# A 128x512 attention loop with three dense steps a round, and gates finished on VectorE where they are made

## The reference, cut to what matters

```python
h = rmsnorm(x, norm1_g[l])
...
o = diff_attention(q, k, vb, lam, slopes)
o = rmsnorm(o, sub_norm_g[l]) * (1.0 - lam_init)
y_b = o.transpose(0, 2, 1, 3).reshape(bsz, s, B_WIDTH)

gates = jax.nn.sigmoid(h @ w_gate[l] + b_gate[l])
g_a, g_b = jnp.split(gates, 2, axis=-1)
merged = g_a * (y_a @ w_up_a[l]) + g_b * (y_b @ w_up_b[l])
x = x + merged @ w_out[l]

h2 = rmsnorm(x, norm2_g[l])
```

## Time and profile before

| | us |
|---|---|
| median of 3 runs | 1771.48 |
| lowest, highest | 1768.0, 1773.71 |
| the profiled execution | 1772.76 |
| its span | 1770.7 |
| PE busy | 1523.5 (86%) |
| DVE busy | 948.3 (54%) |
| ACT busy | 714.9 (40%) |

### The profile page before, as it was taken

The page is one execution under the profiler, slowest core; times in us unless marked ns, Lnnn a source line. Parts: engine busy times, 40 slices in busy tenths (PEclk is TensorE's granted clock), DMA queues, the critical chain, the costliest instruction groups (busy, mean ns, idle before and its releaser), DMA issues.

```text
span 1770.7 us, 17596 instructions
## 1 busy us (share of the span) xinstructions
PE 1523.5 (86%) x7159; PEld 1147.0 (65%) x7159; DVE 948.3 (54%) x1301; ACT 714.9 (40%) x1043; POOL 68.2 (4%) x80
## 2 busy tenths in 40 slices
PE   5999997798786963899999991989697899999999
PEld 4888775586565842555555551868585877678887
DVE  3444246623763445788888874675545535321334
ACT  4333334424443220666666662244322215652231
POOL 1000000000000000111011101000000000000000
PEclk9999998998997986899999996999897988999999
DMA  6422221122104430999999984220101003002241
GB/s 197 168 96 75 96 73 66 68 75 72 70 26 161 152 119 23 307 327 340 331 336 335 329 294 156 72 71 26 47 1 48 1 24 119 1 1 72 95 143 48
DMA packets 80348, 224.01 MB, mean 127 GB/s; under 512 B 9044, under 2 KB 10182, under 8 KB 76167
## 3 DMA queue, kind: packets, MB, share of 16 engines
q1 hardware_dynamic: 71558, 193.73, 32.3%
q0 software_dynamic: 6144, 20.71, 3.5%
q10 hardware_dynamic: 2560, 8.39, 1.3%
HBM read 200.00 MB, written 22.81 MB: 126 GB/s over the span
## 4 chain that ended last, share of the span: by engine, by line
PE 59%; DVE 25%; ACT 11%; DMA 2%; issue 2%; SPq 1%; POOL 0%; DVEq 0%; POOLq 0%; ACTq 0%
PE PS L502 14%; PE PS L504 14%; PE PS L503 14%; DVE wlo L1152 7%; DVE htlo L1152 5%; PE PS L928 4%; ACT whi L1950 3%; PE PS L499 3%; DVE ylo L1152 2%; ACT work L1950 2%; PE PS L1077 2%; ACT yhi L1950 2%; PE PS L1068 1%; ACT hthi L1950 1%; DVE work L1561 1%
## 5 line engine op out<-in xcount | busy, mean ns | idle before, releaser
L1152 DVE TENSOR_TENSOR wlo<-raw,whi 128x2048 fp32r<-128x2048 f32 x74 | 169.1, 2291 | 356.3 <-ACT whi L1950 356.3
L1950 ACT ACTIVATE whi<-raw 128x2048 fp32r<-128x2048 f32 x74 | 141.2, 1912 | 334.9 <-PE PS L504 333.5
L499 PE MATMUL PS<-consts,work 128*128 128x128 f32 (+1 forms) x652 | 100.7, 298 | 125.9 <-DVE work L1178 53.2
L502 PE MATMUL PS<-whi,hthi 128*128 128x512 f32 x480 | 200.1, 417 | 9.2 <-ACT work L1950 6.4
L502 PE MATMUL PS<-hthi,whi 128*128 128x512 f32 x480 | 198.3, 413 | 5.1 <-ACT scratch L1950 2.8
L503 PE MATMUL PS<-wlo,hthi 128*128 128x512 f32 x480 | 190.9, 398 | 0.0
L504 PE MATMUL PS<-whi,htlo 128*128 128x512 f32 x480 | 190.8, 398 | 0.0
L504 PE MATMUL PS<-hthi,wlo 128*128 128x512 f32 x480 | 190.0, 396 | 0.0
L503 PE MATMUL PS<-htlo,whi 128*128 128x512 f32 x480 | 189.5, 395 | 0.0
L499 PEld LDWEIGHTS PS<-consts,work 128*128 128x128 f32 (+1 forms) x652 | 85.2, 182 | 155.1 <-DVE work L1178 54.4
L1950 ACT ACTIVATE work<-PS 128x512 f32<-128x512 f32 (+3 forms) x204 | 103.3, 531 | 88.6 <-PE PS L992 51.2
(11 more groups left out here) (320 smaller groups left out, 2600.3 us busy)
## 6 DMA issues: line engine op xcount, KB each, us to landing
raw<-in_w_in SPq DMA_DIRECT2D x44, 1024.0 KB
raw<-in_w SPq DMA_DIRECT2D x80, 512.0 KB
scratch<-in_w SPq DMA_DIRECT2D x48, 512.0 KB
raw<-in_w SPq DMA_DIRECT2D x19, 1024.0 KB
scratch<-in_w SPq DMA_DIRECT2D x13, 1024.0 KB
raw<-in_w_gate SPq DMA_DIRECT2D x8, 1024.0 KB
raw<-in_w_out SPq DMA_DIRECT2D x8, 1024.0 KB
y_scratch<-work ACTq DMA_DIRECT2D x32, 256.0 KB, 7.1
```

What stands on the lines that cost most here:

```text
L499: return e.transpose(o, i, ident[0:n, 0:n])
L502: e.matmul(o, lh, rh, start=start, stop=False)
L1152: tt(lo, raw_place(j), as_f32(hi), SUB).then_inc(*ve.mark("lo", j))
L1950: return e.activation(o, i, f, bias=bias, scale=scale)
```

## The change

The loop has 20 rounds and advances the generator three times in each. What is left of it runs behind the loop, and only then comes `finish` of the last head. DVE has its third advance behind `combine`.

ACT no longer copies a gate chunk; it writes exp(-(x + bias)), with the negated bias made once in `nbg`. DVE adds 1 and takes the reciprocal (`gate_sum`), one step into the next chunk, the last one in the last gap. In the first half DVE then multiplies `mg` by it (`gated`) and nothing is stored. In the second half POOL stores it after the reciprocal. The merge loads one set instead of two, and has no sigmoids.

```diff
-    gate_dram = nc.dram_tensor("gate_scratch", [2, KD, P, SEQ], F32, kind="Internal").ap()
+    gate_dram = nc.dram_tensor("gate_scratch", [KD, P, SEQ], F32, kind="Internal").ap()
...
-    g2p = small(KD)
+    g2p, nbg = small(KD), small(2 * KD)
...
# tensor
-            for n in range(STEPS + 5):
+            for n in range(STEPS + 4):
                 if n < STEPS:
                     scores(half, n)
-                next(beside, None)
                 next(beside, None)
                 if 0 <= n - 2 < STEPS:
                     turn_weights(half, n - 2)
...
             for _ in beside:
                 pass
+            finish(half, STEPS - 1)
...
# vector
+            ts(nbg, bg, -1.0, None, MUL).then_inc(*ve.mark())
...
+        def gate_sum(half, k):
+            tmp = merge_tmp[:, k % 2, :]
+            on.wait_ge(*ac["out", ("ga", "gb")[half], k // HB, k % HB])
+            ts(tmp, tmp, 1.0, None, ADD).then_inc(*ve.mark())
+            settle()
+            e.reciprocal(tmp, tmp).then_inc(*ve.mark("gate", half, k))
+
+        def gated(k):
+            settle()
+            on.wait_ge(*ac["out", "ua", k // HB, k % HB])
+            tt(mg[:, k, :], mg[:, k, :], merge_tmp[:, k % 2, :], MUL).then_inc(*ve.mark("gated", 0, k))
+
         def beside_attention(half):
             for b in range(2):
                 for c in range(HB):
+                    k = b * HB + c
                     for kk in range(KD):
+                        if kk == 1 and k:
+                            gate_sum(half, k - 1)
+                        if kk == 2 and k and half == 0:
+                            gated(k - 1)
                         yield
                 for step in range(GAP):
                     if step in (0, 2):
                         split()
+                    if step == 4 and b:
+                        gate_sum(half, KD - 1)
+                        if half == 0:
+                            gated(KD - 1)
                     yield
...
-            for n in range(STEPS + 5):
+            for n in range(STEPS + 4):
                 if n < STEPS:
                     scores(half, n)
-                next(beside, None)
                 next(beside, None)
                 if 0 <= n - 3 < STEPS:
                     normalise_head(half, n - 3)
                 next(beside, None)
-                next(beside, None)
                 if 0 <= n - 1 < STEPS:
                     combine(half, n - 1)
+                next(beside, None)
                 if 0 <= n - 5 < STEPS:
                     finish(half, n - 5)
             for _ in beside:
                 pass
+            finish(half, STEPS - 1)
...
# vector, merge_second
-                    on.wait_ge(*ac[event, "gate"])
+                    on.wait_ge(*(gate_got["all"] if name == "ub" else ac[event, "gate"]))
+                    if name == "ub":
+                        on.wait_ge(*gate_put[k % 2][KD - 2 + k % 2])
...
-        for k in range(KD):
-            on.wait_ge(*ac["gate a", k])
-            tt(mg[:, k, :], mg[:, k, :], gate_a[:, k, :], MUL).then_inc(*ve.mark())
-        ve.also("first merged 1")
...
# scalar, gate_chunk
-            if half or k > 1:
-                on.wait_ge(*gate_put[k % 2][half * KD + k - 2])
-            else:
-                on.wait_ge(*ve["dist"])
-                on.wait_ge(*yz_put["all"])
-            act(merge_tmp[:, k % 2, :], inside(name, b, c), ACT.Copy).then_inc(*ac.mark("out", name, b, c))
+            on.wait_ge(*ve["gains"])
+            on.wait_ge(*yz_put["all"])
+            if half == 0 and k > 1:
+                on.wait_ge(*ve["gated", 0, k - 2])
+            elif half:
+                on.wait_ge(*(gate_put[k % 2][k - 2] if k > 1 else ve["gated", 0, KD - 2 + k]))
+            act(merge_tmp[:, k % 2, :], inside(name, b, c), ACT.Exp, bias=nbg[:, half * KD + k:half * KD + k + 1],
+                scale=-1.0).then_inc(*ac.mark("out", name, b, c))
...
# scalar, the same rounds as above, and
-        on.wait_ge(*gate_got["all"])
-        for k in range(KD):
-            act(gate_a[:, k, :], gate_a[:, k, :], ACT.Sigmoid, bias=bg[:, k:k + 1]).then_inc(*ac.mark("gate a", k))
-        for k in range(KD):
-            act(gate[:, k, :], gate[:, k, :], ACT.Sigmoid, bias=bg[:, KD + k:KD + k + 1]).then_inc(*ac.mark())
-        ac.also("merged", "gate")
...
# gpsimd
-        for half, name in enumerate(("ga", "gb")):
-            for k in range(KD):
-                on.wait_ge(*ac["out", name, k // HB, k % HB])
-                e.dma_start(gate_dram[half, k], merge_tmp[:, k % 2, :]).then_inc(*gate_put[k % 2].mark(half * KD + k))
+        for k in range(KD):
+            on.wait_ge(*ve["gate", 1, k])
+            e.dma_start(gate_dram[k], merge_tmp[:, k % 2, :]).then_inc(*gate_put[k % 2].mark(k))
...
# sync
-        e.dma_start(gate_a, gate_dram[0].rearrange("k p n -> p k n")).then_inc(*gate_got.mark("first"))
-        e.dma_start(gate, gate_dram[1].rearrange("k p n -> p k n")).then_inc(*gate_got.mark("all"))
+        e.dma_start(gate, gate_dram.rearrange("k p n -> p k n")).then_inc(*gate_got.mark("all"))
...
-        on.wait_ge(*ve["first merged 1"])
+        on.wait_ge(*pe["ub", 1, HB - 1])
+        on.wait_ge(*ve["attention"])
         e.dma_start(xw, xv).then_inc(*xw_got.mark("all"))
```

More of the change, by code:

```diff
@@ L274, in build @@
     gate = W[:, 0:2, :].rearrange("p a n -> p (a n)").rearrange("p (k n) -> p k n", k=KD)
-    gate_a = W[:, 2:4, :].rearrange("p a n -> p (a n)").rearrange("p (k n) -> p k n", k=KD)
     h2t = W[:, 2:4, :].rearrange("p a n -> p (a n)").rearrange("p (k n) -> p k n", k=KD)
@@ L2575, in sync @@
         e.dma_start(wr[:, :, NG:], w_re[0].rearrange("(k p) n -> p k n", p=P)).then_inc(*wr_got.mark("all"))
-        on.wait_ge(*gate_put[0][2 * KD - 2])
-        on.wait_ge(*gate_put[1][2 * KD - 1])
-        e.dma_start(gate_a, gate_dram[0].rearrange("k p n -> p k n")).then_inc(*gate_got.mark("first"))
-        e.dma_start(gate, gate_dram[1].rearrange("k p n -> p k n")).then_inc(*gate_got.mark("all"))
+        on.wait_ge(*gate_put[0][KD - 2])
+        on.wait_ge(*gate_put[1][KD - 1])
+        e.dma_start(gate, gate_dram.rearrange("k p n -> p k n")).then_inc(*gate_got.mark("all"))
         first_out = unit["wo", 0][0]
```

## The result

| | before | after |
|---|---|---|
| median, us | 1770.28 (4 runs) | 1803.32 (4 runs, 1799.35 to 1808.44) |
| ratio after to before | | 1.0181, 95% interval 1.0157 to 1.0205 |
| profiled execution, us | 1772.76 | 1805.49 (span 1803.8) |
| DVE busy, us | 948.3 | 1006.9 |
| ACT busy, us | 714.9 | 703.5 |

The change makes the kernel 33 us slower; 1804 us was forecast. Three windows over the changed part answer to the earlier trace rows: stretch, length, busy time and instructions of PE, PEld, DVE, ACT and POOL, granted clock, DMA share and GB/s.

What follows compares the result with a forecast made beforehand. Loops bound by a ring of PE scores, DVE maximum, ACT exponentials, DVE combine and PE transposes, with DVE late. 1772.76 + 7.6 + 40.4 - 13.7 - 1.3 = 1805.8, less 1.3: 1804 us; range 1785 to 1824.

Steps and rivals of the forecast that it cites:

- Part 1: Attention loops: three dense steps (three matmuls each) a round instead of four cost +3.8 us a half, +7.6 us for both.
- Waits for L1294: In each loop, PE's waits for the last DVE instruction of combine grow by 7.1 us a half.
- the end: Behind each loop, the 7.8 us wait for the scaled last head becomes 4.5 us for the split: 3.3 us gained.
- The sixteen dense steps: Behind the loop, sixteen dense steps (10.9 us) run before the last head's transposes and cover its square, root and scaling.
- Part 2: Gates on DVE in the loops: ten gate sums of 3.67 us plus 3.6 us of products, together +40.4 us.
- the exposure: In each loop, five gate sums stand between a maximum and combine, each paid in full: 18.4 us a half.
- no cover: DVE's idle time before combine hides none of the gate sums; up to 5 us a half kept for the low end.
- My check against the sigmoids: ACT's gate exponential costs nothing over the 0.60 us copy, since sigmoids of that shape take 9.91 / 16 = 0.62 us.
- The clock: Rival: five longer PE waits a half each add up to 1 us through slower matmuls, 1814 us; chance 0.08.
- Part 3: Merge: w_up_b product loses its idle PE and slow matmuls, -13.7 us; the second norm's table load goes, -1.3 us.
- The slope: DVE's 128x512 reciprocal: 6 ns for each further element, from medians at 2 and 4 elements, gives 3.2 us.
- the two medians: Reciprocals of 166 ns for 2 elements a partition and 178 ns for 4, compared because both start after a wait.

Runs made afterwards that it cites:

- e_act3c: Changed kernel (three steps a round) with gates finished on ACT, plus, in the middle gap, high parts behind a round's exponentials and low parts behind a combine: 1763.59 us, ratio 0.9921.
- the rounds alone: Kernel before with only the changed rounds (three dense steps a round, 20 rounds, rest behind the loop), gates as before: 1782.95 us, ratio 1.0042.
- e_act4c: Kernel before's rounds, gates finished on ACT, end splits behind the last head's scaling, middle-gap DVE low parts three advances after ACT's high parts: 1755.43 us, ratio 0.9873.
- e_act4: Changed kernel with gates finished on ACT (exponential, logarithm, exponential) and the rounds of before, four advances a round: 1762.26 us, ratio 0.9902.
- e_sizes: Changed kernel with each chunk's reciprocal made in 1, 2, 4, 8 or 16 pieces, 512 to 32 elements a partition: 1803.48 us in one run.

## Why the prediction was right

**Part 1, the rounds.** Forecast +3.8 us a half, measured +4.7 and +4.2 us. Waits for L1294 grew by 8.0 us in the first half (7.1 forecast), the end gained 3.4 us (3.3 forecast), and the late thing there is the split's low part after 4.4 to 4.5 us, as forecast. Wrong was the place: I spread the growth over all waiting rounds, and three fifths of it sat in the two rounds with splits. With the splits apart the first loop keeps about 0.8 us of the cost and the second about 3.6 us, by the estimate from e_act3c, so how much the other rounds pay stays open. The sixteen dense steps in front of the last head's transposes were also a miscount: sixteen advances lie behind the loop and six of them are empty; from the last product with v on it is fourteen steps, which still cover the head's chain.

**Part 2, the gates.** The term was 40.4 us, all of it waits. Against the rounds alone the loops grew by 20.2 and 13.8 us, 34.0 us, and only 13.6 + 9.4 = 23.0 us of that is idle time of PE; the other 6.6 + 4.4 = 11.0 us are longer busy time (the clock, below). The reciprocal was nearly right (3.35 us for 3.2), the exposure was not: of five gate sums in the second loop (5 x 3.82 = 19.1 us) 9.4 us show as idle time of PE, 13.8 us with its longer busy time. Two steps of the forecast failed. I placed every sum between a maximum and a `combine`; the ones at steps 17 and 47 of the generator stand behind the `combine`, ahead of the next scores. And "no cover" was too hard: DVE's waits in front of L1288 are 10.8 and 11.5 us with the rounds alone and 8.9 and 9.3 us with the gate sums, so some 2 us a half were hidden there. (The fall from the 13.2 us of the earlier trace rows is larger, but about half of it comes with the rounds.) Where the rest of the 19.1 us went was not followed. ACT's exponential with a bias takes 687 ns, not the 597 of the copy that I put at nothing; it is 0.09 us, 16 times. My check against the sigmoids misread their row: 9.91 / 16 = 0.62 us is the distance from one to the next, and one takes 708 ns. ACT's groups by form in the first loop of e_act4c show it, with the logarithm above it and the second exponential below:

```profile
L1961 ACT ACTIVATE scratch<-scratch,consts 128x512 f32<-128x512 f32 x8 | 5.8, 723 | 0.3
L1961 ACT ACTIVATE scratch<-PS,smalls 128x512 f32<-128x512 f32 x8 | 5.5, 687 | 15.4 <-PE PS L503 15.4
L1961 ACT ACTIVATE scratch<-scratch 128x512 f32<-128x512 f32 x8 | 5.0, 631 | 0.3
```

**The clock** was a rival with a chance of 0.08, and its 10 us are there: PE is busy 6.7 us longer in the first loop and 4.4 us in the second for the same matmuls. Without it the waits for L1294, +21.4 us in the first half, less the end's 3.3 us, would give +18.1 us; 24.9 us were measured. The sum did not reach the rival's 1814 us because the waits grew by less than forecast. The argument against it, that slow work in a waiting round is free, did not hold. A reason may be that some of it runs ahead of the scores on which DVE waits; which of the slow work counts was not isolated.

**Part 3, the merge.** Forecast -13.7 us, measured 59.00 - 46.15 = -12.9 us (-13.1 us in e_act4), and the table load -1.29 us. Nothing took the place of the wait: the gates' load was issued 8.7 us after PE began the product (590.65 against 581.91), and PE never waited for the unit issued behind it.

**The slope.** 3.2 us came from 12 ns between 2 and 4 elements, and e_sizes says that this was luck in part. A line of 6.36 ns an element and 95 ns gives 108 and 121 ns there. The two of 4 elements take 178 ns, those of 2 elements 106 to 168 ns by what stands in front of them, so a fixed time that depends on the neighbour covers the slope at these sizes. My reason for the two medians was wrong as well: I said that both operations start after a wait, but the two of 4 elements have 0.0 us idle before them. The sign of the slope was sound (a streaming operation adds 2 ns), its size was not to be trusted as far as I did. By the Trainium skill's repeat count of 8 (VectorE: DVE Perf Modes, First, the fixed hardware budget), read as eight passes, an estimate is 4.3 us; a pass is put at the 1.05 ns that an element adds to a product here (692 ns for 512 and 161 ns for 4). The trace does not agree: it has 3353 ns, about six such passes.

**The sum.** +8.9 for the rounds (7.6 forecast), +34 for the gates (40.4), -14.2 for the merge and the norm (15.0) is +28.7 us. The 33 us of the medians hold 4 us more, no more than executions differ by in the unchanged stretches. That 1804 us was forecast and 1803 us came is luck: the waits behind the gates were put at 40.4 us and are 23.0 us, the clock was put at nothing and costs 11.0 us, and the 4 us fill the rest. What the prediction had right is that a 128x512 reciprocal on DVE takes over 3 us, that it stands in the ring, and that its cost is larger than what the merge gains.

## What to carry to other kernels

An engine that is busy for 65% of a loop has little room if it sits in the loop's ring: of 19.1 us put between steps of the ring 13.8 us were paid here, whatever the busy share says, so new work belongs on the engine that idles in the ring, or behind the step that others wait for. Look up a new instruction's price per element before moving a function to another engine; here the same gate costs 3.8 us on DVE or two ACT instructions of 0.6 to 0.7 us, and all of the gates on ACT lengthen a half by 2 us. And take the cost of a stage of preparation (here loads and sixteen sigmoids behind the loop) apart from the rearrangement that is meant to hide it: the merge gained its 13 us with either.

## What the runs showed of the hardware

DVE's RECIPROCAL on float32 costs 6.36 ns for each element of a partition from 32 to 512 elements; 128x512 take 3353 ns where a product of the same shape takes 692 ns, almost five times as long. For 2 elements it takes 106 ns right behind another, long reciprocal and 167 ns after a wait. ACT's ln and exp in place over 128x512 take 723 and 631 ns; the ln has a bias from a column and the exp has none. Between exp with such a bias and a copy without, both from PSUM, the difference is 90 ns too (687 and 597 ns). Longer waits of PE in a loop went with a lower granted clock (0.92 to 0.83) and longer busy time, 83.5 to 90.2 us for the same matmuls, and taking out the reciprocal alone gave 3.7 us of it back. The mean clock does not tell that cost: with the rounds alone it is 0.87 and PE is busy for 83.6 us.
